# Four strips of a projection in seven block products instead of eight, in a two-block kernel on one core

## The reference

```python
h = rms_norm(x, norm1_g[l])
z = h @ w_in[l]                      # 1024 x 4608
u_pool, u_lru, u_gate = z[..., :o1], z[..., o1:o2], z[..., o2:o3]
g_a = jax.nn.sigmoid(z[..., o3:o4])
g_b = jax.nn.sigmoid(z[..., o4:])
y_a = pooling_mixer(u_pool, ...) @ proj_a[l]
y_b = rglru_mixer(u_lru, u_gate, ...) @ proj_b[l]    # ends in h * gelu(u_gate)
x = x + (g_a * y_a + g_b * y_b) @ w_out[l]
...                                  # norm, router, 16 experts (top 2), second mixer, expert-choice FFN
```

## Time and profile before

| | |
|---|---|
| median of three runs | 2052.35 us (2047.5 to 2056.64) |
| profiled execution | 2050.1 us, its span 2048.7 us |
| busy in the span | PE 1880.1 us (92%), weight loads 763.0, DVE 491.1 (24%), ACT 276.2 (13%), POOL 33.7 |
| chain that ended last | PE 64%, DMA 29%, DVE 4% |
| mean granted clock of TensorE | 0.98 of full |
| DMA | 589.8 MB, mean 288 GB/s |

### The profile page before, as it was taken

The page is one execution under the profiler, slowest core; times in us unless marked ns, Lnnn a source line. Parts: engine busy times, 40 slices in busy tenths (PEclk is TensorE's granted clock), DMA queues, the critical chain, the costliest instruction groups (busy, mean ns, idle before and its releaser), DMA issues.

```text
span 2048.7 us, 19408 instructions
## 1 busy us (share of the span) xinstructions
PE 1880.1 (92%) x8418; PEld 763.0 (37%) x8418; DVE 491.1 (24%) x965; ACT 276.2 (13%) x498; POOL 33.7 (2%) x44
## 2 busy tenths in 40 slices
PE   8999999999999989999998999888888888888886
PEld 4444444453333335554444333222222222222222
DVE  5456000331101037970213011111101111110112
ACT  3222000121010126303111000000000000000001
POOL 0000000001000010000000000000000000000000
PEclk9999999999999999999999999999999999999998
DMA  6121032448999962112257999999999999999996
GB/s 257 64 82 41 0 123 82 181 158 325 407 410 392 402 219 83 42 41 77 82 226 295 410 427 428 428 428 428 427 427 428 428 428 428 427 428 427 427 429 272
DMA packets 68537, 589.80 MB, mean 288 GB/s; under 512 B 5472, under 2 KB 6880, under 8 KB 37216
## 3 DMA queue, kind: packets, MB, share of 16 engines
q1 hardware_dynamic: 59904, 556.55, 65.9%
q10 hardware_dynamic: 4448, 17.28, 2.1%
q0 software_dynamic: 4096, 14.68, 2.1%
HBM read 575.91 MB, written 12.58 MB: 287 GB/s over the span
## 4 chain that ended last, share of the span: by engine, by line
PE 64%; DMA 29%; DVE 4%; issue 1%; ACT 1%; POOL 0%; DVEq 0%; ACTq 0%
PE ps L250 25%; DMA ring<-in_w_up 22%; PE ps L1045 12%; PE ps L2217 8%; PE ps L2191 6%; DMA ring<-in_w_down 5%; PE ps L674 3%; PE ps L1835 3%; PE ps L264 2%; PE ps L596 1%; PE ps L1726 1%; PE ps L2172 1%; DMA AR<-h_rows,AR 1%; DVE XT L2329 0%; PE ps L1066 0%
## 5 line engine op out<-in xcount | busy, mean ns | idle before, releaser
L250 PE MATMUL ps<-AR,ring 128*128 128x512 f32 x1160 | 501.6, 593 | 3.4 <-DVE AR L2047 2.4
L250 PEld LDWEIGHTS ps<-AR,ring 128*128 128x128 f32 x1160 | 220.1, 190 | 278.7 <-issue 275.3
L2191 PE MATMUL ps<-AR 128*64 128x512 f32 x1040 | 236.5, 600 | 36.9 <-DMA AR<-in_w_up 26.3
L2329 DVE TENSOR_TENSOR XT<-XT,ps 128x512 f32<-128x512 f32 x128 | 81.9, 684 | 783.6 <-PE ps L2172 783.6
L2191 PE MATMUL ps<-ring,AR 128*64 128x512 f32 x1008 | 231.0, 601 | 40.8 <-DMA ring<-in_w_up 31.0
L1045 PE MATMUL ps<-ring,AR 128*32 128x512 f32 x1536 | 249.4, 597 | 3.0 <-ACT AR L1193 2.0
L2191 PEld LDWEIGHTS ps<-AR 128*64 128x64 f32 x1040 | 72.3, 137 | 193.5 <-issue 121.6
L2191 PEld LDWEIGHTS ps<-ring,AR 128*64 128x64 f32 x1008 | 68.7, 137 | 200.1 <-issue 115.7
L1045 PE MATMUL ps<-AR 128*32 128x512 f32 x768 | 125.1, 595 | 0.0
L2217 PE MATMUL ps<-AR 128*64 128x512 f32 x512 | 123.2, 636 | 0.8 <-ACT AR L2254 0.7
L2217 PE MATMUL ps<-ring,AR 128*64 128x512 f32 x512 | 119.2, 610 | 4.5 <-DMA ring<-in_w_down 3.3
(11 more groups left out here) (352 smaller groups left out, 1086.4 us busy)
## 6 DMA issues: line engine op xcount, KB each, us to landing
AR<-in_w_gate SPq DMA_DIRECT2D x33, 2048.0 KB, 33.6
ring<-in_w_up SPq DMA_DIRECT2D x32, 2048.0 KB, 35.4
AR<-in_w_up SPq DMA_DIRECT2D x32, 2048.0 KB, 33.5
ring<-in_w_down SPq DMA_DIRECT2D x32, 2048.0 KB, 35.4
AR<-in_w_down SPq DMA_DIRECT2D x32, 2048.0 KB, 35.4
ring<-in_w_gate SPq DMA_DIRECT2D x31, 2048.0 KB, 35.0
ring<-in_w_in SPq DMA_DIRECT2D x15, 2048.0 KB, 9.0
ring<-in_exp_w_gate SPq DMA_DIRECT2D x15, 2048.0 KB, 8.2
```

Of the source, the lines that this page charges most:

```text
L250: x = PE.matmul(ps, l, r, start=i == 0, stop=i == len(pairs) - 1)
L2191: x = PE.matmul(GU[2 * m + f // 2][64 * (f % 2):64 * (f % 2) + 64, :], XS[n // 2 % 2][:, k * P + 64 * b:k * P + 64 * b + 64], w[:, kk_, f ...
L2329: DV.tensor_tensor(XK[:, o:o + T], XK[:, o:o + T], co_bank(i)[:, :], ALU.add).then_inc(d_co, 1)
```

## The change

The strips g1, ga1, gb0 and gb1 are no longer computed tile by tile. A pair of tiles (128 columns `lo` and 128 columns `hi` of a strip, 256 columns apart) times the 512 tokens is taken as a 2x2 by 2x2 block product, halves of 4 k-blocks and halves of 256 tokens, and computed from seven products with sums ahead and behind. One product is four k-blocks against 256 token columns. Eight pairs p = 0 to 7: p 0, 1 are g1 (gelu), 2, 3 ga1, 4, 5 gb0, 6, 7 gb1. g0 and ga0 stay as they were; ga0's four tiles with their ya tiles now come where `gate(1)` was, and g1 after them. The sigmoids of ga go to `M` instead of `TM`. Sums ahead: four of the tokens' tile (`h_sums`, 4x256 columns each) and four for each strip (`w_sum`, the same size). Sums behind: five per pair on DVE, after a copy by ACT. PE's order is now: wr/wi of the second half; ga0 and ya tiles 0 to 3; pairs 0, 1; pairs 2, 3, each followed by two ya tiles; pairs 4 to 7, each followed by two yb tiles; output tiles.

```diff
-        load("g1", kcols(win, 2048, 512), s_g, 8)
+        load("ga0", kcols(win, 2560, 512), s_ga, 4)
         load("pa", krows(A["proj_a"], 0, 4), s_ya, 8)
-        load("ga0", kcols(win, 2560, 512), s_ga, 4)
-        load("ga1", kcols(win, 3072, 512), s_ga, 8)
-        load("gb0", kcols(win, 3584, 512), s_gb, 4)
+        load("g1", kcols(win, 2048, 512), s_pp, 14)
+        load("ga1", kcols(win, 3072, 512), s_pp, 28)
+        load("gb0", kcols(win, 3584, 512), s_pp, 42)
         load("pb0", kcols(A["proj_b"], 0, 512), s_yb, 4)
-        load("gb1", kcols(win, 4096, 512), s_gb, 8)
+        load("gb1", kcols(win, 4096, 512), s_pp, 56)
...
# act_front, in the loop of the square roots
+                    if half and j == 2:
+                        AC.wait_ge(s_ga, 1)
+                        AC.wait_ge(s_zz, 4)
+                        AC.activation(M[:, sl(0)], bank[ga_bank(0)][:, :], ACT.Copy).then_inc(s_gas, 1)
...
+            for p in range(8):
+                lo, hi, _ = st_tiles(p)
+                AC.wait_ge(s_pp, 7 * p + 1)
+                if p < 2:
+                    AC.wait_ge(s_ybo, 4)
+                elif p in (4, 5):
+                    AC.wait_ge(s_ybo, 8)
+                elif p > 5:
+                    AC.wait_ge(s_m2, 2 * p - 10)
+                AC.activation(lo[:, 0:256], bank[st_banks(p)[0]][:, 0:256], ACT.Copy).then_inc(s_pa, 1)
+                AC.wait_ge(s_pv, 5 * p + 5)
+                for v in (hi, lo):
+                    AC.activation(v, v, ACT.Gelu_apprx_tanh if p < 2 else ACT.Sigmoid).then_inc(s_pa, 1)
...
+        def st_banks(p):
+            return (4, 5, 7) if p % 2 == 0 else (1, 2, 3)
...
# pe_front
-            gate(1)
...
+            for c in range(4):
+                PE.wait_ge(*((s_sg, 13), (s_sg, 15), (s_gas, 1), (s_gl, 2))[c])
+                matmuls(bank[ga_bank(c)][:, :], cols(w, c * P, HT, KT)).then_inc(s_ga, 1)
+                PE.wait_ge(*((s_sg, 14), (s_sg, 16), (s_gl, 1), (s_gl, 3))[c])
+                matmuls(bank[ya_bank(c)][:, :], cols(pa, c * P, YP, 4)).then_inc(s_ya, 1)
...
+                def product(ps, h, a, b):
+                    o = p % 2 * P
+                    x = matmuls(ps[:, 256 * h:256 * h + 256], [(a[:, k, o:o + P], b[:, k, :]) for k in range(4)])
+                    x.then_inc(s_pp, 1)
+                if p == 0:
+                    PE.wait_ge(s_gl, 4)
+                    PE.wait_ge(s_gas, 4)
+                    PE.wait_ge(s_ht, 4)
+                elif p == 1:
+                    PE.wait_ge(s_m, 4)
+                    PE.wait_ge(s_gas, 5)
+                else:
+                    PE.wait_ge(s_pv, 5 * p - 5)
+                if p % 2 == 0:
+                    PE.wait_ge(*strip(p // 2)[1:])
+                product(r1, 0, a11, HB_[0][0])
+                PE.wait_ge(s_ws, 4 * (p // 2) + 4)
+                product(r2, 0, z2, t2)
+                product(r3, 0, z1, t1)
+                product(r3, 1, z3, t3)
+                PE.wait_ge(s_pa, 3 * p + 1)
+                product(r1, 1, a12, HB_[1][0])
+                PE.wait_ge(s_pv, 5 * p + 1)
+                product(r2, 1, a22, t4)
+                product(r2, 0, z4, HB_[1][1])
...
# out_tile: the wait of the first tile, k in the order in which M's tiles come
+                for j, k in enumerate((2, 0, 3, 1, 6, 4, 7, 5)):
                     if i == 0:
-                        PE.wait_ge(s_m2, k + 1)
+                        PE.wait_ge(s_m2, j + 1)
...
# dve_front, second half of the recurrence, between the conv and L800
+                if half:
+                    h_sums()
+                    for i in range(4):
+                        w_sum(0, i)
...
+            for c in range(4):
+                if c == 3:
+                    for i in range(4):
+                        w_sum(1, i)
+                DV.wait_ge(s_gas, c + 2)
+                merged(c, c)
+            for p in range(8):
+                DV.wait_ge(s_pp, 7 * p + 2)
+                DV.wait_ge(s_pa, 3 * p + 1)
+                DV.tensor_tensor(hi[:, 256:512], lo[:, 0:256], r2[:, 0:256], ALU.add).then_inc(s_pv, 1)
+                DV.wait_ge(s_pp, 7 * p + 4)
...
+                DV.tensor_tensor(mid, ..., r3[:, :]..., ALU.add).then_inc(s_pv, 1)            # 512 columns
+                DV.tensor_tensor(hi[:, 256:512], hi[:, 0:256], r3[:, 0:256], ALU.add).then_inc(s_pv, 1)
+                DV.wait_ge(s_pp, 7 * p + 5)
+                DV.tensor_tensor(lo[:, 0:256], lo[:, 0:256], r1[:, 256:512], ALU.add).then_inc(s_pv, 1)
+                if p in (1, 2):
+                    w_sum(2, 2 * p - 2)
+                    w_sum(2, 2 * p - 1)
+                DV.wait_ge(s_pp, 7 * p + 7)
+                DV.tensor_tensor(mid, mid, r2[:, :]..., ALU.add).then_inc(s_pv, 1)            # 512 columns
+                if p in (4, 5):
+                    w_sum(3, 2 * p - 8)
+                    w_sum(3, 2 * p - 7)
+                for i, c in enumerate(reversed(st_cols(p))):
+                    DV.wait_ge(s_pa, 3 * p + 2 + i)
...                                       # gated (p < 2), merged (p < 4), else the two operations of L835 and L838
```

More of the change, by code:

```diff
@@ L303, in build @@
         gr0 = area(D)
+        sums = area(2048)
+        ST = [v[:, 1024 * i:1024 * i + 1024].rearrange("p (k t) -> p k t", k=4) for v in (U, sums) for i in range(2)]
+        HB_ = [[HT[:, 2048 * i:2048 * i + 2048].rearrange("p (k t) -> p k t", k=4)[:, :, 256 * j:256 * j + 256]
+                for j in range(2)] for i in range(2)]
+        s0 = x0 + 4 * 515
+        SETS = [[AR[:, o:o + 1024].rearrange("p (k t) -> p k t", k=4) for o in at_] for at_ in (
+            (X4 + CH + 2048, X4 + CH + 3072, N1), (s0, s0 + 1024, s0 + 2048), (s0 + 3072, s0 + 4096, s0 + 5120))]
+        SETS.append(SETS[1])
+        STRIPS = ("g1", "ga1", "gb0", "gb1")
         UP = [M[:, 528 * g:528 * g + 528] for g in range(4)]
@@ L377, in build @@
         s_bt, s_hid, s_gl, s_ybo = sem("dve_b"), sem("dve_hidden"), sem("act_gelu"), sem("dve_yb")
-        s_gas, s_m, s_gbs, s_m2 = sem("act_ga"), sem("dve_ma"), sem("act_gb"), sem("dve_mb")
+        s_gas, s_m, s_m2 = sem("act_ga"), sem("dve_ma"), sem("dve_mb")
+        s_ht, s_ws, s_pa, s_pv = sem("dve_h_sums"), sem("dve_w_sums"), sem("act_sevenths"), sem("dve_sevenths")
         s_rp, s_ra, s_rv = sem("pe_router"), sem("act_router"), sem("dve_router")
@@ L395, in sp_front @@
                     SP.wait_ge(s_ri, 16)
+                    SP.wait_ge(s_pp, 14)
                 sp_load(n)
@@ L460, in act_front @@
                     AC.activation(T2[:, sl(j)], T2[:, sl(j)], ACT.Sqrt, scale=4.0).then_inc(s_rt, 1)
-            for c in range(8):
-                AC.wait_ge(s_g, c + 1)
[L463 to L468, removed]
-                AC.wait_ge(s_ga, c + 1)
[L470 to L483, removed]
+                    if half and j == 2:
+                        AC.wait_ge(s_ga, 1)
+                        AC.wait_ge(s_zz, 4)
+                        AC.activation(M[:, sl(0)], bank[ga_bank(0)][:, :], ACT.Copy).then_inc(s_gas, 1)
@@ new lines, in act_front @@
+            for c in range(4):
+                AC.wait_ge(s_g, c + 1)
+                AC.wait_ge(s_bt, 4 + c + 1)
+                AC.activation(TM[c], bank[g_bank(c)][:, :], ACT.Gelu_apprx_tanh).then_inc(s_gl, 1)
+            AC.wait_ge(s_gas, 1)
+            AC.activation(M[:, sl(0)], M[:, sl(0)], ACT.Sigmoid).then_inc(s_gas, 1)
+            for c in range(1, 4):
+                AC.wait_ge(s_ga, c + 1)
+                AC.activation(M[:, sl(c)], bank[ga_bank(c)][:, :], ACT.Sigmoid).then_inc(s_gas, 1)
@@ L484, in act_front @@
+            AC.wait_ge(s_pp, 56)
             AC.wait_ge(s_xk, G_ROW + 2)
@@ L544, in g_bank, with ga_bank, ya_bank, st_cols @@
             return (33 + c) % 8
[L546 to L550, removed]
+        def ga_bank(c):
+            return (5, 7, 5, 2)[c]
+        def ya_bank(c):
+            return (6, 0, 1, 3, 0, 0, 6, 6)[c]
+        def st_banks(p):
+            return (4, 5, 7) if p % 2 == 0 else (1, 2, 3)
+        def st_cols(p):
+            c = p % 2 + (0 if p in (4, 5) else 4)
+            return c, c + 2
+        def st_tiles(p):
+            c = st_cols(p)[0]
+            v, o = (M, c * T) if p in (2, 3) else (tm, c % 4 * T)
+            return v[:, o:o + T], v[:, o + 1024:o + 1536], v[:, o + 256:o + 1280].rearrange("p (q t) -> p q t", t=256)[:, 0::3, :]
+        def strip(b):
+            w, s, n = weights(STRIPS[b], 8)
+            return [[w[:, 4 * i:4 * i + 4, 256 * j:256 * j + 256] for i in range(2)] for j in range(2)], s, n
         def x_bank(i):
@@ L602, in pe_front, with gate @@
                 matmuls(b[:, :], [(p1("poolw", g * P, P), Z[:, sl(g)])]).then_inc(s_yp, 1)
-            def gate(half):
-                w, s, n = weights(f"g{half}", 8)
+            def gate():
+                w, s, n = weights("g0", 8)
                 PE.wait_ge(s, n)
[L607 to L610, removed]
+                for c in range(4):
```

(115 more changed lines are left out.)

2 lines of the change are left out of this document (1 added, 1 removed).

## The result

The changed kernel took 2038.84 us in the median of four runs (2035.59 to 2040.89) against 2051.9 for the kernel before; the ratio is 0.9934, 95% interval 0.9908 to 0.9961, so 13.1 us faster where 14.2 were forecast. Its profiled execution had a span of 2038.4 us, against 2048.7.

The account below looks back on a forecast made before the run. PE was taken to bound the touched mixer, DMA the kernel's end. Products -13.1 us and the pb0 wait -1.1, all other terms 0, sum to -14.2 us: 2038.1 us from a median of 2052.35, range 2031 to 2047.

Parts of the forecast that it names:

- What bounds: Touched mixer bound by PE, kernel's end by DMA; matmul time removed before 371.64 us starts all that follows earlier.
- Products: Four strips: 256 matmuls of 512 columns become 448 of 256 at 0.216 us each, worth -13.1 us.
- Weight loads: In the strips' products, loads rise from 256 to 448 but fit under the matmuls: cost 0.
- The rule named against it: Trainium skill: weight loads overlap running matmuls only where row groups differ, so the 192 added loads would stand in the open.
- pb0: PE's 1.09 us wait for the pb0 transfer at the first gb tile vanishes behind pair 4: -1.1 us.
- ga0 ahead of g1: Moving ga0 and its ya tiles before g1 causes no waits; pair 0 starts at 191.6 us: cost 0.
- Sums ahead: DVE's `h_sums` and `w_sum(0)`, 8 x 1.23 = 9.8 us, hide in 19.84 us idle behind the conv, 10 us over.
- Inside a pair: DVE's first sum ends at about 4.2 us, due at 8.6 for the sixth product; over 4 us in hand, cost 0.
- The second rival: Handovers hold PE in the pairs: 3.5 us each gives 2066 us; 2% for slower, 7% for part of gain lost.
- What follows: Behind the output tiles all hangs on PE's progress; the 400 MB stream starts 14 us earlier and lasts as long.
- the first rival: The gain is lost in the DMA-bound part from 1266 us: no change, 2050 to 2054 us; 5%.
- The forecast of the same 14 us at every mark behind: Output tiles, first experts, last DMA-bound stretch and end all come 14 us earlier.

Follow-up runs that it names:

- `eighth`: Changed kernel with an eighth product per pair (product two computed twice): 2049.69 us against 2050.3 for the kernel before, ratio 0.9997.
- `order_alone`: Changed kernel's order and transfers, but each pair's tiles computed directly by 2 x 8 products of 512 columns, without sums: 2049.15 us against 2050.3 before, ratio 0.9995.
- `narrow`: Changed kernel with each 256-column product issued as two of 128 (896 instructions and weight loads for 448): 2038.78 us against 2047.78 before, ratio 0.9955.
- `late2`: Changed kernel with two unused 3072-column reduces on VectorE ahead of each pair's first sum: 2062.69 us, ratio 1.007 to the kernel before.
- the first pair: First profiles of changed kernel and kernel before (2038.84 against 2051.9 us); the second pair repeats both unchanged: 2038.05 against 2050.3 us, ratio 0.9949.
- `late1`: Changed kernel with one unused 3072-column reduce on VectorE ahead of each pair's first sum: 2033.03 us against 2047.78 before, ratio 0.9926.

## Why the prediction was right

- **What bounds.** Right. Between u1 and the output tiles there was only PE, and what was taken from PE or added to it moved the start of the output tiles as the counts and distances of instructions say: 13.17 us for 13.16 in the changed kernel, 13.81 for 13.8 in `eighth`. The page's digits were read too sharply: they say 90% or more for DMA in slices 23 to 39 and 6 tenths in the last, not 99% in the last fifteen; nothing hangs on it.
- **Products.** -13.1 us, measured 13.17 (`order_alone` to changed). The distance at 256 columns was read off neighbours as 0.216 and is 0.2159. Half of a 512-column instruction, 0.2146, would have given 0.6 us too much of gain.
- **Weight loads.** Cost 0, right; `narrow` doubles them once more and adds 3.4 us. The rule named against it stands in a section that also has another case, by which the loads need not stand in the open; the prediction gave only the first.
- **pb0.** -1.1, measured 1.3 in `order_alone`: the restart behind the gap goes as well.
- **ga0 ahead of g1.** Cost 0, right. Pair 0 began at 190.04 us (product two at 191.77 less 1.73), forecast 191.6 less the 1.57 by which that execution was early.
- **Sums ahead.** 1.22 to 1.23 us each, hidden with 10.24 us over; forecast 10.
- **Inside a pair.** The number was right for another reason. I had DVE's first sum end at 4.2 us because of the tail of the pair before; it ends at 4.1 because it waits for product two, and the tail is over by then. The slack of 4.5 us lies between 3.35 and 6.7 by the two late kernels, and the wait of 2.1 in `late2` puts it at 4.6.
- **The second rival's price.** Too low. I had 13.8 us of loss against before (2066 us) for 3.5 us of wait in each pair; 2.1 us already gave 14.9, since most stops of PE cost clock too, a term that the price did not have. The point from which it decides stood (4 us forecast, 4.6 measured); the price per microsecond of wait is 27.4 / 16.9 = 1.6.
- **What follows.** Its mean length is the same with and without the gain (1678.8 us), so the first rival, a gain lost in the DMA-bound part, falls for anything like the whole gain. Medians moved by 13.1 and 12.3 us where the path moved by 14.5. The first is inside its interval; the second is 2.2 us short, and its interval ends at 14.1, just below the path's 14.5. The place near 800 us may have a part in it; it is not explained further. The forecast of the same 14 us at every mark behind was too sharp for one profile: 16.2, 8.7 and 10.3 us in the first pair, 16.7, 14.0 and 13.1 in the second.

## What to carry to other kernels

Trading eight block products for seven pays here as nearly 1/8 of the matmul time (13.2 of 109.9 us) because the distance between float32 matmuls is linear in the columns down to 256, and because every sum fell into idle time of another engine: check both from rows, the distance from neighbours in width and the idle time by who ends it. Read the slack of each handover from its due time and leave some over, since stops of 2.1 us per pair turned 13 us of gain into 15 us of loss. To judge a change of half a per cent, compare the touched stretch between two marks of the trace: here it repeats to 0.1 us, where the rest of the kernel moves by 6.7 us from one execution to the next.

## What the runs showed of the hardware

- A float32 128x256 matmul instruction with its own weight load comes every 0.2159 us, a 128x128 one of the same products every 0.1116 (`narrow`), while the turns' come every 0.109; I expected one value for both.
- Stops of 2.1 us on PE were followed by a fall of the granted clock in five of eight cases (0.92 over 205 to 220 us, 0.91 over 220 to 240) and not in three (1.00 between 240 and 260 us). A stop with a fall cost 4.06 us in all, one without 2.38.
- The clock also falls without a stop of PE: sixteen 128x512 matmuls behind 32 of 16 columns took 8.3 to 10.0 us in seven of nine profiles and 6.98 in two, in kernels with and without the change. The granted clock over these sixteen was 0.71 in the first profile of the changed kernel (1068 to 1078 us, 9.87 us) and 1.00 in that of `late1` (1067 to 1074 us, 6.98 us).
